# Two transformer blocks on one core: first weights of a stage split earlier, modulation steps in another order and other stages

## The reference, cut to what matters

```python
def _modulate(x, cond, norm_g, w_ada, b_ada):            # layers ev and od
    mod = jax.nn.silu(cond) @ w_ada + b_ada
    shift, scale, gate = jnp.split(mod[:, None, :], 3, axis=-1)
    return rmsnorm(x, norm_g) * (1.0 + scale) + shift, gate
...
def layer_ab(x, c, ...):                                 # layer l0
    sh_m, sc_m, g_m, sh_f, sc_f, g_f = adaln(c, mod_w, mod_b)
    h = modulate(x, norm_mix, sh_m, sc_m)
    (a_gate, a_x, q, kc, vc, ks, vs, kw, vw, gts) = _split_2(h @ w_in, IN0_SIZES)
    y_a = rg_lru(causal_conv(a_x, conv_w, conv_b), ...) * jax.nn.gelu(a_gate)
    y_b = nsa_mixer(q, kc, vc, ks, vs, kw, vw, jax.nn.sigmoid(gts), ...)
    x = x + g_m[:, None, :] * (jnp.concatenate([y_a, y_b], axis=-1) @ w_out)
    h = modulate(x, norm_ffn, sh_f, sc_f)
    return x + g_f[:, None, :] * swiglu(h, wg, wu, wd)
...
def layer_c(x, c, ...):                                  # layer l1, same frame
    q, k, v, q_idx, k_idx, w_idx = _split_2(h @ w_in, IN1_SIZES)
    x = x + g_m[:, None, :] * (dsa_mixer(q, k, v, q_idx, k_idx, w_idx) @ w_out)
    ...
```

## Time and profile before

| | |
|---|---|
| Runs | 2526.53, 2530.59, 2533.37 us (median 2530.59) |
| Profiled execution | 2528.26 us, of which the span on the core is 2526.4 us |
| Mean granted TensorE clock | 0.958 |
| TensorE busy | 93% of the span |
| VectorE, ScalarE, GpSimd busy | 52%, 31%, 13% |

### The profile page before, as it was taken

The page is one execution under the profiler, slowest core; times in us unless marked ns, Lnnn a source line. Parts: engine busy times, 40 slices in busy tenths (PEclk is TensorE's granted clock), DMA queues, the critical chain, the costliest instruction groups (busy, mean ns, idle before and its releaser), DMA issues.

```text
span 2526.4 us, 30550 instructions
## 1 busy us (share of the span) xinstructions
PE 2340.3 (93%) x11882; PEld 1774.8 (70%) x11882; DVE 1304.8 (52%) x2847; ACT 790.8 (31%) x1671; POOL 337.8 (13%) x345
## 2 busy tenths in 40 slices
PE   7899999989999989979898989999988688999997
PEld 6766575578547566868765868888776467788876
DVE  4564746622454438365856266663437863433333
ACT  4154004411113017231447122223423361222233
POOL 2300100000100210020100110004521001000044
PEclk9999999989999999987979999999979899999999
DMA  7200330001240640033310135553213102222222
GB/s 288 92 18 18 125 117 34 2 16 63 92 150 1 156 147 3 32 119 126 118 34 2 67 124 176 184 188 128 93 66 118 51 1 67 100 97 89 99 100 75
DMA packets 58267, 225.89 MB, mean 89 GB/s; under 512 B 20478, under 2 KB 21118, under 8 KB 41740
## 3 DMA queue, kind: packets, MB, share of 16 engines
q1 hardware_dynamic: 58124, 223.94, 26.3%
HBM read 221.83 MB, written 2.10 MB: 89 GB/s over the span
## 4 chain that ended last, share of the span: by engine, by line
PE 77%; DVE 13%; DMA 3%; POOL 3%; ACT 2%; issue 2%; SPq 0%; POOLq 0%; DVEq 0%; ACTq 0%
PE PS L86 72%; PE PS L91 5%; DVE ACC L115 2%; DMA ADA<-in_l_mod 1%; DVE RINGr L103 1%; POOL WKr L103 1%; DVE WK L157 1%; DVE WK L108 1%; DVE WK L142 1%; DVE SM L152 1%; DVE WK L115 1%; DMA WK<-in_rpb 1%; ACT WK L98 1%; POOL Xr L103 1%; DVE WK L103 1%
## 5 line engine op out<-in xcount | busy, mean ns | idle before, releaser
L86 PE MATMUL PS<-Hr,GBr 128*128 128x512 f32 x1280 | 443.9, 400 | 25.7 <-DVE RINGr L103 20.4
L86 PE MATMUL PS<-Hr,RINGr 128*128 128x512 f32 x1040 | 406.5, 391 | 0.0
L96 ACT ACTIVATE WK<-PS 128x512 f32<-128x512 f32 (+3 forms) x390 | 189.8, 518 | 528.9 <-PE PS L86 326.7
L115 DVE SCALAR_TENSOR_TENSOR ACC<-ADA,SM,ACC 128x256 f32<-128x256 f32 x608 | 293.0, 505 | 91.5 <-DMA ACC<-in_l_mod_b 47.7
L86 PE MATMUL PS<-H,RING 128*128 128x512 f32 (+1 forms) x928 | 337.2, 515 | 0.0
L86 PEld LDWEIGHTS PS<-Hr,GBr 128*128 128x128 f32 x1280 | 243.8, 191 | 86.8 <-DVE RINGr L103 22.1
L103 DVE TENSOR_TENSOR RINGr<-RING,GBr 128x1024 fp32r<-128x1024 f32 (+1 forms) x155 | 199.3, 1324 | 165.5 <-ACT GBr L96 165.5
L86 PEld LDWEIGHTS PS<-H,RING 128*128 128x128 f32 x928 | 172.3, 191 | 135.0 <-issue 127.1
L86 PE MATMUL PS<-RING,GB 128*128 128x256 f32 x1156 | 252.8, 381 | 3.5 <-DVE GB L120 2.2
L86 PEld LDWEIGHTS PS<-RING,GB 128*128 128x128 f32 x1156 | 220.6, 191 | 34.4 <-issue 4.1
L86 PEld LDWEIGHTS PS<-Hr,RINGr 128*128 128x128 f32 x1040 | 199.2, 192 | 41.4
(11 more groups left out here) (192 smaller groups left out, 2933.9 us busy)
## 6 DMA issues: line engine op xcount, KB each, us to landing
ADA<-in_l_mod SPq DMA_DIRECT2D x96, 512.0 KB, 3.7
RING<-in_l_gu SPq DMA_DIRECT2D x44, 1024.0 KB, 4.9
RING<-in_l_wd SPq DMA_DIRECT2D x24, 1024.0 KB, 5.0
RING<-in_l_in SPq DMA_DIRECT2D x17, 1024.0 KB, 5.2
RING<-in_ev_in SPq DMA_DIRECT2D x13, 1024.0 KB, 5.8
ADA<-in_od_ada SPq DMA_DIRECT2D x24, 512.0 KB, 3.6
RING<-in_od_in SPq DMA_DIRECT2D x11, 1024.0 KB, 5.9
RING<-in_l_out SPq DMA_DIRECT2D x8, 1024.0 KB, 5.0
```

The source lines that it names most:

```text
L86: self.last = self.eng.matmul(out, lhsT, rhs, start=start, stop=stop, skip_group_check=True)
L96: self.last = self.eng.activation(out, in_, func, bias=bias, scale=scale)
L115: self.last = self.eng.scalar_tensor_tensor(out=out, in0=a, scalar=s, in1=b, op0=op0, op1=op1)
```

## The change

1. `ADA_ORDER`: the list is walked in another order. Each stage's gate groups (4, 5) come later, behind the shift and scale groups of the stage that follows.
2. The calls of `ada` stand elsewhere. New: four steps in each of the first four tiles of out ev, three in each of the first three tiles of out od, four in each of the first three tiles of out l0. Gone: ten calls in proj l0m (13 chunks, c71 to c83) and four in proj I (8 chunks, c132 to c139). The ffn loops take up to four steps an iteration where they took three: in ffn l0 an odd f has an apply and three chunks, an even f one chunk and a sum. On SyncE the calls in out od and out l0 stand ahead of the four `load()` of the stage that follows.
3. The first weights chunk of proj l0m and of both ffns is split in the last tile of the output projection before: ScalarE rounds between its two halves of the norm, VectorE subtracts between its two adds. The first chunk of l1 (`l1_vw`) is split at the end of ffn l0. At f == 3 of the norm stands now the second chunk.
4. In the stages of 512 columns GpSimd lowers the blocks 0, 2, 4, 6 and VectorE 1, 3, 5, 7.
5. VectorE lowers z = 40 and 41 too. The first final norm's weights lie in H, where GB's place is now used for a split.

```diff
+ADA_ORDER = (("ev", range(6)), ("od", range(4)), ("l0m", range(4)), ("od", (4, 5)), ("l0f", range(4)), ("l0m", (4, 5)),
+             ("l1m", range(4)), ("l0f", (4, 5)), ("l1f", range(4)), ("l1m", (4, 5)), ("l1f", (4, 5)))
...
+            elif name == "l1_vw":
+                place = GBr[:, 15360:15904] if h else EXQr[:, 0:544]
...
+        def hl_signal(st, k, gi):
+            return dve_value if (gi == 0 if wide(st) else k % 2) else pool_value
...
         def al_signal(z):
-            return dve_value if z > 41 else pool_value
+            return dve_value if z > 39 else pool_value
...
-            out_proj("od_out", range(4), lambda k: None)                 # TensorE
+            out_proj("od_out", range(4), lambda k: None, lambda t: ada(3) if t < 3 else None)
...
                     fm_split("l0m", FIRST["l0_in1"] + j, m, "ag", t, gated("ag", t))
-                    ada(2)
...
                 for f in range(8):                                       # VectorE, norm_mod
...
-                        if wide(st) and gi == 1:
-                            lower(f)
+                    if f > 1 and f % 2 == 0:
+                        lower(f - 1)
+                    elif f == 7:
+                        lower(7)
                     if f == 3 and st != "ev":
-                        rest({"l0m": FIRST["l0_in1"], "l0f": FIRST["l0_gu"], "l1m": FIRST["l1_vw"],
-                              "l1f": FIRST["l1_gu"]}[st])
+                        rest({"l0m": FIRST["l0_in1"] + 1, "l0f": FIRST["l0_gu"] + 1, "l1m": FIRST["l1_vw"] + 1,
+                              "l1f": FIRST["l1_gu"] + 1}[st])
...
                     for jj in range(2):                                  # VectorE, out_proj
+                        if jj and t == tiles[-1] and nxt is not None:
+                            rest(FIRST[nxt])
                         add(name, st, t, jj, where["out", name, t, jj], cds[0] if t < 4 else cds[1], 2 * n + jj)
...
-                    ada(3)                                               # all engines, ffn
+                    ada(4)
...
-                        for z in (42, 43):
+                        for z in range(40, 44):
...
             def twice(t):
                 final_norm("fin1", t)
                 norm_tile("l0m", t)
+                if t < 3:
+                    ada(3)
-            out_proj("od_out", "od", range(4), ("c",), twice)
+            out_proj("od_out", "od", range(4), ("c",), twice, "l0_in1")
...
             ada_until(ADA_AFTER["od", 5])                                # SyncE
             since(sp, "att N")
-            sp.dma_start(GB[:, 15104:16128], brow(A["fin1"], 1024)).then_inc(fin_in["fin1"], "fin1", 16)
+            sp.dma_start(H[:, 0:1024], brow(A["fin1"], 1024)).then_inc(fin_in["fin1"], "fin1", 16)
+            for t in range(3):
+                ada(3)
             for j in range(4):
                 load()
             cur.allowed |= {"l0f"}
             ada_until(ADA_AFTER["l0m", 3])
-            for j in range(4):
-                ada(2)
-                ada(2)
-                load()
...
```

More of the change, by code:

```diff
@@ L221, in _ada_steps @@
     i = 0
-    for st, (w, c0, cds, g) in STAGES.items():
-        for grp in range(6):
+    for st, groups in ADA_ORDER:
+        w, c0, cds, g = STAGES[st]
+        for grp in groups:
             for j in range(2):
@@ L1480, in round_h @@
                     if f == 3 and st != "ev":
-                        round_chunk({"l0m": FIRST["l0_in1"], "l0f": FIRST["l0_gu"], "l1m": FIRST["l1_vw"],
-                                     "l1f": FIRST["l1_gu"]}[st])
+                        round_chunk({"l0m": FIRST["l0_in1"] + 1, "l0f": FIRST["l0_gu"] + 1, "l1m": FIRST["l1_vw"] + 1,
+                                     "l1f": FIRST["l1_gu"] + 1}[st])
             def copy_out(tag, t, s0, n):
@@ L2251, in ffn @@
                             dve.then_inc(dve_value, ("al", wd, z))
+                        if st == "l0f":
+                            rest(FIRST["l1_vw"])
                     for t in range(4):
@@ L2603, in vector, with normed_l0 @@
             since(dve, "att S")
-            out_proj("l0_out", "l0m", range(4), ("c2",), lambda t: norm_tile("l0f", t))
+            def normed_l0(t):
+                norm_tile("l0f", t)
+                if t < 3:
+                    ada(4)
+            out_proj("l0_out", "l0m", range(4), ("c2",), normed_l0, "l0_gu")
             cur.allowed |= {"l1m"}
@@ L2669, in vector @@
             since(dve, "att D")
-            out_proj("l1_out", "l1m", range(4), ("c2",), lambda t: norm_tile("l1f", t))
+            out_proj("l1_out", "l1m", range(4), ("c2",), lambda t: norm_tile("l1f", t), "l1_gu")
             close(of_dve, "out l1")
@@ L2735, in lower @@
             def lower(st, gi, a, b):
-                for f in range(8):
+                for f in range(8) if wide(st) else range(0, 8, 2):
                     own()
@@ L2760, in ffn @@
                 for f in range(22):
-                    ada(3)
+                    ada(4)
                 ada_until(ADA_AFTER[st, 5])
-                for fz in range(42):
+                for fz in range(40):
                     own()
@@ L2889, in gpsimd @@
             since(pool, "norm l0m")
-            for t in range(8):
-                ada(2)
-            for j in range(2):
-                ada(2)
             for m in range(2):
@@ L3040, in sync @@
             ada_until(ADA_AFTER["od", 3])
+            for t in range(4):
+                ada(4)
             for j in range(4):
@@ L3067, in sync @@
             ada_until(ADA_AFTER["l0m", 3])
-            for j in range(4):
-                ada(2)
-                ada(2)
-                load()
-            for j in range(2):
-                load()
-                ada(2)
-            for j in range(2):
+            for j in range(8):
                 load()
@@ L3090, in sync @@
                 load()
-            for j in range(2):
-                ada(3)
-                ada(3)
-                load()
-            for j in range(4):
+            for j in range(6):
                 load()
```

62 lines of the change are left out of this document (37 added, 25 removed).

## The result

The change takes 2542.40 us (median of 8 runs, 2539.39 to 2549.37) where the kernel before takes 2530.74 (8 runs). The ratio is 1.0052, 95% interval 1.004 to 1.0065: slower by 0.5%, some 12 us by the medians and 13 by the ratio. The forecast was 2533 and "same" as the likeliest outcome; the time lies in its range, and the sign is that of its 0.30.

A forecast was written before the change was run, and what follows sets the result against it. The prediction took TensorE's products and the gaps in them to bound the kernel. Losses of 35.3 us against gains of 31.9 made it 3.4 slower, 2533 us, range 2517 to 2547 (2526 to 2541 for the sum itself).

The forecast's parts named there:

- rival 4: Proj l0m and proj I: half of the removed waits come back as others, 2543 us; chance 0.07.
- rival 3: Each new stall costs more than itself, or VectorE's lowerings slow beside GpSimd: 2545 us or above; chance 0.20.
- (b): Start of ffn l0: the 3.99 wait for a chunk's split goes, with some clock behind it; 5.7 us gained.
- (g): Out od: ring load stands behind modulation reloads, so the last tile's add comes late; 9.2 us lost.
- (h): Out l0: ring load stands behind modulation reloads, so the last add ends late; 8.1 us lost.
- (i): Ffn loops: a bias and three chunks in one iteration stall TensorE 2.25 us, six times; 13.5 us lost.
- (e): Ends of both ffns: VectorE lowering z = 40, 41 saves 1.4 us each; 2.8 us gained.
- (f): Starts of four norms: first chunk ready early, but block 7's lowering sets the start; together 1.2 us gained.
- (a): Proj l0m: waits for modulation sums and the slow clock behind them go; 10.8 us gained, 7.3 without the clock.
- (c): Proj I: the 9.88 wait for the last modulation sum goes, about 1.0 stays; 8.9 us gained.
- Rival 1: Ffn loops: the bias lands early and the stalls don't come; 2518 us, faster; chance 0.20.
- Rival 2: Out od and out l0: the ring loads' delays cost nothing; 2516 us, faster; chance 0.08.

The follow-up runs named there:

- Experiment 4: The change with SyncE's four ring loads in out od and out l0 ahead of the reloads for tile 2's last chunks: 2531.52 us, 1.0008.
- experiment 2: The change with three modulation steps an ffn iteration (two chunks and two) in place of four: 2528.81 us, 0.9999.
- experiment 1: The change with ScalarE's round of l1_vw no longer waiting for TensorE's last chunks of ffn l0: 2525.22 us, 0.999.
- experiments 6 and 9: 6: the change with edits of Experiment 4, experiment 2, experiment 1, second chunk split behind the norm's eighth block, 2484.06 us; 9: best_of_all, 2479.56 us.
- three_tile2: The change with edits of Experiment 4, experiment 2, experiment 1, without modulation in the third tiles of out od and out l0: 2501.26 us, 0.989.
- best_of_all: three_tile2 with the second weights chunk also split behind the norm's eighth block in place of the fourth: 2479.56 us, 0.9813.
- experiment 3: The change with SyncE issuing an ffn iteration's bias DMA ahead of its 1 MB ring load: 2526.94 us, 0.9997.
- experiment 10: The change with edits of Experiment 4, experiment 2, experiment 1; 512-column lowerings all on GpSimd: 2510.94 us; instead z = 40, 41 on GpSimd: 2510.41 us.

## Why the prediction came out as it did

**The total: in part luck.** In the span 11.5 us were lost where I had 3.4, and 2542.4 lies past 2541, where the range of my own sum ended. A loss of 14.7 that no term held was partly made up by gains that I had sized too small. That the time is near rival 4's 2543 and rival 3's 2545 says nothing for either.

**Right, with sizes.** (b), (d), (g) and (h) came by the mechanisms named, within 0.6 us a line. (i) came so in its two lines of stalls, 1.6 and 1.2 above the sum; its third line, f = 21, has another cause (below). Experiment 4 takes most of (g) and (h) away, experiment 2 takes (i). Two side sums were off. In (g) I held that with the load in its place the split would be ready by 1077.6 and cost nothing; in experiment 4 the load is in its place, and VectorE is done with the split at 1080.75, since ScalarE's round stands behind its norm half. And in (i) the other price, 2.0 for the bias and 3.2 for the chunk, gives T + 11.0 and no stall at all, not 0.2. (e) saved 1.2 of waits where I had 1.4; with the slow clock that had stood behind the wait of 2.33 (0.50 from 1828 to 1831 before), the lead fell by 3.1 in ffn l0 and 1.7 in ffn l1.

**The step that failed is (f)**, and in it "The new first chunk is ready early", where it is applied to norm l1m. I priced what the second chunk adds to the norm (1.9; measured 0.3), and took the early split of `l1_vw` for free. I had not asked what ScalarE's round waits for: `SPLIT_BEFORE` ties it to one of the last chunks of the down projection, and it waited until TensorE's last product. To ask what is queued behind that wait, as I had asked for the added steps, would have found four adds and their norms. It cost 14.7 by the trace and 15.7 when taken away (experiment 1), more than the whole difference of 12 to 13 us.

**(f) in the other three norms: the size near, the path wrong.** I had 0.3, 1.6 and 1.2 won, with block 7's lowering as what comes last; measured are 1.9, 2.7 and 1.6. But VectorE's four lowerings took 1.32, 0.68, 0.69 and 0.69 in norm l0m, not 1.2 each, and TensorE waits for block 3 instead, behind the second chunk's split. That "almost nothing is gained" was therefore no property of the norm: with that split behind block 7 the same early split is worth 12 us in three stages (experiments 6 and 9).

**Under-sized gains.** (a) with norm l0m brought 15.1 for 11.1, and (c) 12.6 for 8.9. In proj l0m the lead falls by 14.4 (1.2 of it is lost again before att S): 7.3 are the waits that I had, 2.9 the slow clock behind the last of them, where I had 3.5, and the other 4 are TensorE's own products for the three sums (1.12, 1.05 and 1.86 in its timeline before), which I had put at nothing. In (c) two such sums leave (1.9), and the slow clock that I had not counted was worth 2.7: in the windows before, the clock is 0.50 from 1920 to 1930, behind the 9.88 wait of the earlier trace rows, and it is 1.00 at this place after the change. The products of the sums are not gone, they stand in other stages: the 1.8 in out ev and proj M, where I had 0.5, are two of them at 0.9.

**Not foreseen, small.** At f = 21 a gate's apply now falls at the end of ffn l0's loop. ScalarE copies the gate before it rounds the first a, so GpSimd's lowering and TensorE are late; the three engines after the change:

```profile
1721.99 0.60 ACT L96 ACTIVATE GATE<-PS 128x512 f32<-128x512 f32 x1 [5.70 <-PE PS L86]
...
1723.25 2.65 POOL L103 TENSOR_TENSOR WKr<-GB,WKr 128x512 fp32r<-128x512 f32 x2 [27.15 <-ACT WKr L96]
...
1724.66 0.47 PE L86 MATMUL PS<-GBr,WKr 128*128 128x512 f32 x1 [2.71 <-POOL WKr L103]
```

It is part of the 4.5 in that line; in three_tile2 and best_of_all, where no apply stands there, the wait is gone. No run adds the moved steps alone to the kernel before, so the gains (a) and (c) rest on the trace.

**The rivals.** Rival 1 (no ffn stalls) did not come, but two lines on SyncE make it true (experiment 3). Rival 2 did not come; with SyncE's order changed 11 of its 17.3 us are had (experiment 4). Rival 3 (a stall costs more than itself) holds in the ffn: five stalls sum to 9.5 us and cost 15.7 by the marks, 13.4 when taken away (experiment 2). Its other half does not: VectorE's lowerings beside GpSimd were no bound, and putting them back on GpSimd was slower (experiment 10). Rival 4 did not come: no wait of the removed sizes came back in proj l0m or proj I.

## What to carry to other kernels

When work is moved ahead of something else on an in-order engine, look up every semaphore that the moved instruction waits for, not only its data: a wait that guards a buffer the instruction no longer uses can hold up all that stands behind it. On a shared DMA queue put first what can go first; a load that waits for the slowest engine belongs behind the small ones that are ready. And a large gain and a large loss may be in one edit: a budget by stretches, from marks that both traces have, finds them where the total says "0.5%".

## What the runs showed of the hardware

- A stall on TensorE of 1.7 to 2.1 us in the ffn cost 3.1 us on average (15.7 for five by the marks; 2.7 by experiment 2). Behind three of the five the windows show a granted clock of 0.65 to 0.70 in the next three us and 0.73 to 0.78 in those after; behind the other two it stayed at 1.00. The lead rose by 3.6 about the stall at 1541.43, with the clock fallen, and by 1.5 about the one at 1567.64, without. Why it fell behind some of them and not behind the others was not settled.
- A 2 KB bias in an otherwise idle queue, in out od of the change, was issued at 1058.15 and VectorE ran on it at 1059.50, within 1.4 us; behind a 1 MB load it took from 1527.95 to 1532.42. The 2.0 us fixed cost that the Trainium skill gives (page "DMA: Bandwidth & Descriptors", section "Anatomy of one DMA — SWDGE (gpsimd) path"; these DMAs are SyncE's) fits neither, and the measurement decides.
- A lowering of VectorE took 1.32 us beside one of GpSimd (at 1097.78) and 0.68 without (at 1104.46): the meeting costs 0.6, not a whole lowering of GpSimd (1.3). The Trainium skill (page "SBUF — State Buffer", section "Who interferes with whom") speaks of an exclusive lock between the two for such operations. The trace does not contradict it: GpSimd's lowering ran from 1097.27 to 1098.54 and had 0.76 left when VectorE's began. As a price in a sum a whole lowering was too high, since only one of VectorE's four lowerings in norm l0m met one of GpSimd's.
